# Product-key experts: both weight streams in 1 MB halves through six half places, where they were 2 MB pieces through three

## The chip, the cores and the metric

One Trainium2 chip, one of its cores. The program is written out instruction by instruction for five engines: TensorE (PE, matmul), VectorE (DVE), ScalarE (ACT), GpSimd (POOL) and SyncE (SP), which issues all loads. The metric is the device time of one launch in microseconds, lower is better.

## What is computed

The reference is two transformer blocks, one after another, in fp32 on 256 tokens of width 1024. The first has two layers, each a mixer (a gated linear recurrence beside sparse attention) and then product-key experts. The second has one layer with latent attention, a second recurrence and 32 gated experts. The change is about the product-key experts, which each of the first block's two layers computes so:

```
def _peer(x, wq, subkeys, u_tab, v_tab):
    ...
    q = (xf @ wq).reshape(T, PEER_HEADS, 2, PEER_KEY_DIM)
    s = jnp.einsum('thcd,ckd->thck', q, subkeys).astype(jnp.float32)
    sv, si = lax.top_k(s, PEER_TOPK)
    ...
    experts = (ea * PEER_KEYS + eb).reshape(T, PEER_HEADS * PEER_TOPK)
    gate = jax.nn.softmax(cv, axis=-1).reshape(T, PEER_HEADS * PEER_TOPK).astype(x.dtype)
    ...
    def one_chunk(args):
        xc, ec, gc = args
        act = jax.nn.gelu(jnp.einsum('cd,ced->ce', xc, u_tab[ec]))
        return jnp.einsum('ce,ced->cd', act * gc, v_tab[ec])
```

T is 256, there are 8 heads, 128 x 128 = 16384 experts and 16 chosen per head. u_tab and v_tab are 16384 x 1024 each, 64 MB a table and layer.

## The kernel before

The kernel does not gather. It reads both tables whole and computes all 16384 experts for all tokens, with a dense gate that is zero where an expert was not chosen. The experts go in 128 chunks of 128.

- The up product of a chunk (pe_stage1) is 8 fp32 matmuls of 256 columns, each of them two records in the trace: 16 records a chunk. ScalarE applies gelu and stores the 128 x 256 result in H, which holds 76 chunks (HELD).
- A build (pe_build) makes the gates of 32 chunks for 16 tokens from one-hot tables that VectorE writes (dve_keys_hot, dve_gates_hot): 48 small matmuls. VectorE then multiplies H by them (dve_gate). There are 64 builds a layer.
- The down product of a chunk (pe_stage2) is 12 matmuls of 512 columns. H and the v chunk are each split in a high part (ScalarE: act_split_p, act_split_v) and a low part (VectorE: dve_split_p, dve_split_v); v_hi has three buffers and v_lo two. So dve_split_v of chunk c waits for the down product of chunk c-2, and act_split_v for that of c-3.

The order of the work is written out by hand and is the same in all engines' programs. First come 50 up chunks (BEFORE), with the first 16 builds among the last 18 of them. Then there are 128 steps c = 0 to 127. Each does the builds due in it, the up chunks of first_at[c] and the down product of chunk c. first_at[c] is 50 + 2c and 51 + 2c as long as H has room (c up to 24), then one chunk a step, and none from c = 53 on. ScalarE and VectorE split chunk c + 2 in step c.

The weights pass through a ring in SBUF: NSLOT = 3 places of PIECE = 4096 columns, 2 MB each (class Slots, line 209). load() (line 300) takes the next place in turn, waits on SyncE until the load's predecessor in that place has been given back, and issues one DMA, which adds 16 to the place's own semaphore when it has landed. SyncE's program is in order: a load whose place is not free holds up every load behind it. All weights of the first block pass this ring, and in the mixed stretch of the steps both tables do. sp_u and sp_v (lines 957 and 961) load a piece of 4 chunks when their c is a multiple of 4; sp_peer has the order: in each step first the up pieces, then the down piece of chunk c + 2. An up piece is given back by TensorE after its fourth chunk (pe_stage1), a down piece by VectorE after the split of its fourth chunk (dve_split_v). A piece lies in memory as 128 rows of 16 KB.

In the second block's experts the ring gets more places in the arena (more_slots, line 2004).

Of the kernel before, what the change touches and what calls it, by code (L numbers as in the profile page):

```python
# [17 lines left out]
NSLOT = 3  # L18
PIECE = 4096
HELD = 76  # L20
# [211 lines left out]

def bc(ap, axis, n):
    ap = ap.unsqueeze(axis)
    shape = list(ap.shape)
    shape[axis] = n
    return ap.broadcast_to(shape)


def build(nc, d, out):  # L240
    with ExitStack() as ctx:
# [50 lines left out]

        ring = Slots([ring_t[:, i * PIECE:(i + 1) * PIECE] for i in range(NSLOT)], at)
        s_ring = [sem(f"ring{i}_landed") for i in range(NSLOT)]
        fills = [0] * NSLOT
# [4 lines left out]
        def load(src, cols, *key):  # L300
            buf, (s, n) = ring.take(*key)
            i = ring.place[key]
            fills[i] += 1
            S.wait_ge(s, n)
            S.dma(buf[:, 0:cols], src, s_ring[i])
            at.put(("landed", key), s_ring[i], 16 * fills[i])
# [136 lines left out]
        def pe_mod(j):  # L443
# [6 lines left out]
            w = ring.of("w_mod", j).rearrange("p (c n) -> p c n", c=8)  # L450
# [106 lines left out]
        def pe_project_out(l, k, yT, *made):  # L557
            P.wait_ge(*at[made])
            P.wait_ge(*at["landed", ("w_out", l, k)])
            w = ring.of("w_out", l, k).rearrange("p (c n) -> p c n", c=4)  # L560
# [8 lines left out]
        def pe_mixing(l):  # L569
# [5 lines left out]
            for j in range(4):  # L575
                P.wait_ge(*at["landed", ("w_inA", l, j)])
                w = ring.of("w_inA", l, j).rearrange("p (c n) -> p c n", c=8)
# [379 lines left out]
        def sp_u(l, c):  # L957
            if c % 4 == 0:
                load(d["peer_u"][l, c // 4], 4096, "u", l, c // 4)

        def sp_v(l, c):
            if c % 4 == 0 and c < 128:
                load(d["peer_v"][l, c // 4], 4096, "vt", l, c // 4)
# [15 lines left out]
        def pe_stage1(l, c):  # L979
            P.wait_ge(*at["landed", ("u", l, c // 4)])  # L980
            if c >= 2:
                P.wait_ge(*at["gelu", l, c - 2])
            w = ring.of("u", l, c // 4).rearrange("p (i c a) -> p i c a", i=4, c=8)
            P.mm(bU[c % 2][:, 0:256], [(w[:, c % 4, dc, :], xT[:, dc, :]) for dc in range(8)])
            P.mark("up", l, c)
            if c % 4 == 3:
                ring.back(P, "u", l, c // 4)
# [22 lines left out]
        def pe_peer(l):  # L1010
            after_stage(P, "mix", l)
            route_banks.restart()
            for j in range(4):
                P.wait_ge(*at["landed", ("wq", l, j)])
                w = ring.of("wq", l, j).rearrange("p (c n) -> p c n", c=8)
# [121 lines left out]
        def dve_split_v(l, c):  # L1137
            w = ring.of("vt", l, c // 4).rearrange("p (i n) -> p i n", i=4)[:, c % 4, :]
# [5 lines left out]
            if c % 4 == 3:  # L1144
                ring.back(V, "vt", l, c // 4)
# [74 lines left out]
        def act_split_v(l, c):  # L1220
            A.wait_ge(*at["landed", ("vt", l, c // 4)])
            if c >= 3:
                A.wait_ge(*at["down", l, c - 3])
            A.act(v_hi[c % 3], ring.of("vt", l, c // 4).rearrange("p (i n) -> p i n", i=4)[:, c % 4, :], ACT.Copy)
            A.mark("v high", l, c)
# [134 lines left out]
        def pe_task(kind, k, ct):  # L1360
            P.wait_ge(*at["landed", ("w_hg", kind, k)])
            w = ring.of("w_hg", kind, k).rearrange("p (c n) -> p c n", c=8)
# [115 lines left out]
        def pe_mixer():  # L1478
# [17 lines left out]
            w = ring.of("w_kvb").rearrange("p (v c n) -> p v c n", v=2, c=2)  # L1496
# [508 lines left out]
        s_ring += [sem(f"ring{NSLOT + i}_landed") for i in range(len(more_slots))]  # L2005
# [29 lines left out]
        def sp_moe():  # L2035
# [5 lines left out]
            for i in range(len(more_slots)):  # L2041
                ring.bufs.append(more_slots[i])
                ring.tenant.append(None)
                fills.append(0)
            ring.n = NSLOT
# [52 lines left out]
        def pe_up(j, i, k, *gathered):  # L2098
            x = xe[i]
            for v in range(2):  # L2100
# [7 lines left out]
                for h in range(2):  # L2108
                    P.wait_ge(*at["landed", ("w_gu", j, v, h)])
                    w = ring.of("w_gu", j, v, h).rearrange("p (c g n) -> p c g n", c=4, g=2)  # L2110
# [21 lines left out]
        def pe_down(j):  # L2132
# [3 lines left out]
            for hf in range(2):  # L2136
                P.wait_ge(*at["landed", ("w_dn", j, hf)])
                w = ring.of("w_dn", j, hf).rearrange("p (f n) -> p f n", f=4)
# [376 lines left out]
        def start_ring():  # L2515
            ring.bufs, fills[:] = ring.bufs[0:NSLOT], [0] * NSLOT
            ring.restart()
# [183 lines left out]
```

## Time and profile before

| | |
|---|---|
| median of 3 runs | 4375.6 us (4365.14 to 4375.74) |
| the profiled execution | 4377.6 us |
| its span | 4375.8 us |
| TensorE matmul busy | 3942.4 us (90%) |
| TensorE weight load busy | 2746.5 us (63%) |
| VectorE busy | 2018.1 us (46%) |
| ScalarE busy | 895.2 us (20%) |
| mean granted clock of TensorE | 0.944 |
| loads of each table | 64 of 2048 KB, 8.7 us (up) and 8.6 us (down) from issue to landing |

The mean over the span says little, since the stages have different limits. Times in the rows count from the span's start. Layer 0's experts run from about 240 to 1280 us, layer 1's from about 1490 to 2530 us, and the second block's experts from 3285 us to the end. Granted clock is the share of full speed (2.4 GHz) that TensorE was given. "Idle before" is the time in which an engine stood still before a row, with the one that released it.

### The profile page before, as it was taken

How to read it: one execution, taken by the hardware profiler on the slowest of the kernel's cores; microseconds unless marked ns; L12 is line 12 of the kernel's file. 1: busy time of each engine (PE TensorE's matmuls, PEld its weight loads, DVE VectorE, ACT ScalarE, POOL GpSimd, SP SyncE). 2: the span in 40 equal slices, each digit the busy share in tenths (PEclk: the TensorE clock that was granted, in tenths of full speed). 3: DMA queues.
4: the chain of work that ended last, by engine and by line, in shares of the span. 5: the costliest groups of instructions: out<-in, count | busy, mean ns of one | idle time of the engine just before them, and what ended most of it. 6: DMA issues, size and time to landing. Idle time of an engine off the chain costs nothing.

```text
span 4375.8 us, 54878 instructions
## 1 busy us (share of the span) xinstructions
PE 3942.4 (90%) x23468; PEld 2746.5 (63%) x23468; DVE 2018.1 (46%) x3441; ACT 895.2 (20%) x1502; POOL 154.4 (4%) x135
## 2 busy tenths in 40 slices
PE   6989999998988899999998979998869999999986
PEld 5778878886777688887876756565643333332333
DVE  4276645748754497255758533355532111111112
ACT  2311111223434111212233421223300000000000
POOL 0000000000000000000000000021200000000000
PEclk9799999999998899999999989999979999999998
DMA  4433323443344333333443331211129999999993
GB/s 182 155 135 138 132 116 131 159 155 135 135 165 155 134 137 125 124 136 135 154 154 123 137 127 49 106 58 58 58 81 413 427 428 427 428 427 428 425 398 145
DMA packets 62282, 846.18 MB, mean 193 GB/s; under 512 B 6800, under 2 KB 8976, under 8 KB 10160
## 3 DMA queue, kind: packets, MB, share of 16 engines
q1 hardware_dynamic: 62032, 842.60, 47.9%
q8 instruction: 187, 3.06, 0.3%
q14 instruction: 63, 0.52, 0.0%
HBM read 841.52 MB, written 1.05 MB: 193 GB/s over the span
## 4 chain that ended last, share of the span: by engine, by line
PE 67%; DVE 15%; DMA 13%; ACT 3%; issue 2%; SPq 0%; POOL 0%; DVEq 0%; ACTq 0%
PE bank L83 65%; DVE arena L119 6%; DMA ring<-in_w_gu_dram 6%; DMA ring<-in_peer_u_dram 3%; DMA arena<-in_w_gu_dram 3%; ACT arena L109 2%; DVE vlo L119 2%; PE bank L96 2%; DVE arena L187 1%; DVE arena L181 1%; DVE arena L193 1%; DVE arena L145 1%; DVE arena L133 1%; DVE arena L125 1%; DVE arena L127 1%
## 5 line engine op out<-in xcount | busy, mean ns | idle before, releaser
L83 PE MATMUL bank<-xT,ring 128*128 128x256 f32 x5120 | 1174.1, 389 | 55.7 <-DMA ring<-in_peer_u_dram 33.4
L83 PEld LDWEIGHTS bank<-xT,ring 128*128 128x128 f32 x5120 | 988.2, 195 | 197.8 <-DMA ring<-in_peer_u_dram 35.9
L83 PE MATMUL bank<-arena 128*128 128x32 bf16 (+7 forms) x9660 | 926.6, 291 | 145.7 <-DVE arena L119 108.5
L83 PEld LDWEIGHTS bank<-arena 128*128 128x128 bf16 (+4 forms) x9660 | 544.4, 126 | 522.9 <-issue 294.5
L83 PE MATMUL bank<-ring,arena 128*64 128x512 f32 (+1 forms) x2304 | 592.5, 606 | 39.5 <-DMA ring<-in_w_gu_dram 33.7
L109 ACT ACTIVATE arena<-bank 128x256 f32<-128x256 f32 (+2 forms) x484 | 223.8, 462 | 1975.2 <-PE bank L83 1484.6
L83 PEld LDWEIGHTS bank<-ring,arena 128*64 128x64 f32 (+1 forms) x2304 | 194.4, 146 | 427.3 <-issue 328.5
L119 DVE TENSOR_TENSOR arena<-arena 128x512 bf16<-128x512 bf16 (+6 forms) x636 | 424.4, 703 | 82.0 <-ACT arena L109 67.9
L119 DVE TENSOR_TENSOR vlo<-ring,vhi 128x1024 fp32r<-128x1024 f32 x256 | 313.2, 1224 | 267.2 <-PE bank L83 249.8
L83 PE MATMUL bank<-vhi,phi 128*128 128x512 f32 x1024 | 432.3, 422 | 0.0
L83 PE MATMUL bank<-vhi,plo 128*128 128x512 f32 x1024 | 406.7, 397 | 0.0
L83 PE MATMUL bank<-vlo,phi 128*128 128x512 f32 x1024 | 406.6, 397 | 0.0
L83 PE MATMUL bank<-arena,ring 128*128 128x256 f32 (+2 forms) x1472 | 363.3, 409 | 26.6 <-issue 14.2
L119 DVE TENSOR_TENSOR arena<-cst,arena 128x2048 bf16<-128x2048 f32 (+1 forms) x257 | 372.4, 1481 | 0.0
L83 PEld LDWEIGHTS bank<-arena,ring 128*128 128x128 f32 (+1 forms) x1472 | 253.1, 188 | 129.0 <-issue 91.4
L109 ACT ACTIVATE arena<-arena 128x512 f32<-128x512 f32 (+7 forms) x202 | 134.4, 666 | 797.8 <-DVE arena L125 619.0
L109 ACT ACTIVATE vhi<-ring 128x1024 fp32r<-128x1024 f32 x256 | 272.0, 1063 | 31.4 <-DMA ring<-in_peer_v_dram 20.3
L119 DVE TENSOR_TENSOR plo<-arena,phi 128x256 fp32r<-128x256 f32 x256 | 107.9, 421 | 318.2 <-ACT phi L109 318.2
L139 DVE COPY arena<-bank 128x256 f32<-128x256 f32 (+4 forms) x124 | 70.3, 567 | 387.9 <-PE bank L83 337.1
L83 PEld LDWEIGHTS bank<-vhi,plo 128*128 128x128 f32 x1024 | 197.1, 192 | 44.0
L83 PEld LDWEIGHTS bank<-vlo,phi 128*128 128x128 f32 x1024 | 198.0, 193 | 40.3
L83 PEld LDWEIGHTS bank<-vhi,phi 128*128 128x128 f32 x1024 | 197.5, 193 | 39.6
(105 smaller groups left out, 1665.9 us busy)
## 6 DMA issues: line engine op xcount, KB each, us to landing
ring<-in_w_gu_dram SPq DMA_DIRECT2D x85, 2048.0 KB, 19.3
ring<-in_peer_u_dram SPq DMA_DIRECT2D x64, 2048.0 KB, 8.7
ring<-in_peer_v_dram SPq DMA_DIRECT2D x64, 2048.0 KB, 8.6
arena<-in_w_gu_dram SPq DMA_DIRECT2D x55, 2048.0 KB, 19.4
ring<-in_w_dn_dram SPq DMA_DIRECT2D x41, 2048.0 KB, 17.9
arena<-in_w_dn_dram SPq DMA_DIRECT2D x29, 2048.0 KB, 20.6
ring<-in_w_hg_dram SPq DMA_DIRECT2D x14, 2048.0 KB, 8.6
ring<-in_w_mod_dram SPq DMA_DIRECT2D x12, 2048.0 KB, 7.8
```

The costliest lines, as they stand in the source:

```text
L83: i = self.e.matmul(o, l, r, start=start, stop=stop)
L96: self.e.transpose(o, src, ident[0:n, 0:n]).then_inc(self.sem, 1)
L109: self.e.activation(o, i, f, scale=scale, **kw).then_inc(self.sem, 1)
L119: self.e.tensor_tensor(o, a, b, op).then_inc(self.sem, 1)
L125: self.e.tensor_scalar(o, a, s1, None, o1).then_inc(self.sem, 1)
L127: self.e.tensor_scalar(o, a, s1, s2, o1, o2).then_inc(self.sem, 1)
L133: self.e.scalar_tensor_tensor(out=o, in0=a, scalar=s, in1=b, op0=o1, op1=o2).then_inc(self.sem, 1)
L139: self.e.tensor_copy(o, i).then_inc(self.sem, 1)
L145: self.e.tensor_reduce(o, i, AX.X, op, negate=neg).then_inc(self.sem, 1)
L181: self.e.max(o, i).then_inc(self.sem, 1)
L187: self.e.max_index(o, v, i).then_inc(self.sem, 1)
L193: self.e.match_replace(o, v, i, by).then_inc(self.sem, 1)
```

## The change

A new class Ring takes the place of Slots for the weight ring. It counts in half places. A load of up to 2048 columns takes one half, a wider one both halves of a place; where a wide load would start on a second half, that half is skipped. load() waits for all that the taken halves held before. Each half has its own landing semaphore (a wide load uses that of its first half). sp_u and sp_v load 2 chunks at a time, 1 MB as 128 rows of 8 KB, when their c is even; the halves are given back after every second chunk. All other loads of the ring keep their size and order. The readers of wide loads now slice the first 4096 columns, which is all that the parts left out here do beside the added places of the second block.

```
@@ -17,6 +17,7 @@
 ALPHA = 4.0 ** 0.25
 NSLOT = 3
 PIECE = 4096
+HALF = PIECE // 2
 HELD = 76
 TURNED = 19
 BEFORE = 50
...
@@ -225,6 +226,37 @@
 
     def of(self, *key):
         return self.bufs[self.place[key]] if key in self.place else self.bufs[0]
+
+    def back(self, q, *key):
+        self.at.put(("back", key), q.sem, q.n)
+
+
+class Ring:
+
+
+    def __init__(self, places, at):
+        self.places, self.at, self.place = list(places), at, {}
+        self.restart()
+
+    def restart(self):
+        self.n, self.tenant = 0, [None] * (2 * len(self.places))
+
+    def take(self, cols, *key):
+        wide = cols > HALF
+        if wide and self.n % 2:
+            self.n += 1
+        i = self.n % len(self.tenant)
+        self.n += 1 + wide
+        before = [k for k in self.tenant[i:i + 1 + wide] if k]
+        self.tenant[i:i + 1 + wide] = [key] * (1 + wide)
+        self.place[key] = i
+        return i, [self.at["back", k] for k in before]
+
+    def half(self, i):
+        return self.places[i // 2][:, i % 2 * HALF:]
+
+    def of(self, *key):
+        return self.half(self.place.get(key, 0))
 
     def back(self, q, *key):
         self.at.put(("back", key), q.sem, q.n)
...
@@ -290,19 +322,19 @@
         def par(c, n=1):
             return pp[:, c:c + n]
 
-        ring = Slots([ring_t[:, i * PIECE:(i + 1) * PIECE] for i in range(NSLOT)], at)
-        s_ring = [sem(f"ring{i}_landed") for i in range(NSLOT)]
-        fills = [0] * NSLOT
+        ring = Ring([ring_t[:, i * PIECE:(i + 1) * PIECE] for i in range(NSLOT)], at)
+        s_ring = [sem(f"ring{i}_landed") for i in range(2 * NSLOT)]
+        fills = [0] * (2 * NSLOT)
         banks = Slots(bank, at)
         s_landed = {}
         s_out = sem("out_stored")
 
         def load(src, cols, *key):
-            buf, (s, n) = ring.take(*key)
-            i = ring.place[key]
+            i, before = ring.take(cols, *key)
             fills[i] += 1
-            S.wait_ge(s, n)
-            S.dma(buf[:, 0:cols], src, s_ring[i])
+            for s, n in before:
+                S.wait_ge(s, n)
+            S.dma(ring.half(i)[:, 0:cols], src, s_ring[i])
             at.put(("landed", key), s_ring[i], 16 * fills[i])
 
         def once(dst, src, *key):
...
@@ -447,7 +479,7 @@
             P.wait_ge(s, n)
             P.wait_ge(*at["landed", ("w_mod", j)])
             P.wait_ge(*at["silu c"])
-            w = ring.of("w_mod", j).rearrange("p (c n) -> p c n", c=8)
+            w = ring.of("w_mod", j)[:, 0:PIECE].rearrange("p (c n) -> p c n", c=8)
             for dc in range(8):
                 for g in range(4):
                     P.one(b[32 * g:32 * g + 32, 0:128], sc[:, dc, :], w[:, dc, g * 128:g * 128 + 128],
...
@@ -955,12 +987,12 @@
                 build_at.setdefault(b + 1, []).append(n)
 
         def sp_u(l, c):
-            if c % 4 == 0:
-                load(d["peer_u"][l, c // 4], 4096, "u", l, c // 4)
+            if c % 2 == 0:
+                load(d["peer_u"][l, c // 4][:, c % 4 * 1024:c % 4 * 1024 + 2048], 2048, "u", l, c // 2)
 
         def sp_v(l, c):
-            if c % 4 == 0 and c < 128:
-                load(d["peer_v"][l, c // 4], 4096, "vt", l, c // 4)
+            if c % 2 == 0 and c < 128:
+                load(d["peer_v"][l, c // 4][:, c % 4 * 1024:c % 4 * 1024 + 2048], 2048, "vt", l, c // 2)
 
         def sp_peer(l):
             for j in range(4):
...
@@ -977,14 +1009,14 @@
 
 
         def pe_stage1(l, c):
-            P.wait_ge(*at["landed", ("u", l, c // 4)])
+            P.wait_ge(*at["landed", ("u", l, c // 2)])
             if c >= 2:
                 P.wait_ge(*at["gelu", l, c - 2])
-            w = ring.of("u", l, c // 4).rearrange("p (i c a) -> p i c a", i=4, c=8)
-            P.mm(bU[c % 2][:, 0:256], [(w[:, c % 4, dc, :], xT[:, dc, :]) for dc in range(8)])
+            w = ring.of("u", l, c // 2)[:, 0:HALF].rearrange("p (i c a) -> p i c a", i=2, c=8)
+            P.mm(bU[c % 2][:, 0:256], [(w[:, c % 2, dc, :], xT[:, dc, :]) for dc in range(8)])
             P.mark("up", l, c)
-            if c % 4 == 3:
-                ring.back(P, "u", l, c // 4)
+            if c % 2:
+                ring.back(P, "u", l, c // 2)
 
         def pe_build(l, n):
             ah, bh = Aoh[n % 2], Boh[n % 2]
...
@@ -1135,14 +1167,14 @@
             V.mark("p split", l, c)
 
         def dve_split_v(l, c):
-            w = ring.of("vt", l, c // 4).rearrange("p (i n) -> p i n", i=4)[:, c % 4, :]
+            w = ring.of("vt", l, c // 2)[:, c % 2 * 1024:c % 2 * 1024 + 1024]
             V.wait_ge(*at["v high", l, c])
             if c >= 2:
                 V.wait_ge(*at["down", l, c - 2])
             V.tt(v_lo[c % 2], w, v_hi[c % 3].bitcast(F32), SUB, lag=FREE)
             V.mark("v split", l, c)
-            if c % 4 == 3:
-                ring.back(V, "vt", l, c // 4)
+            if c % 2:
+                ring.back(V, "vt", l, c // 2)
 
         def dve_peer(l):
             after_stage(V, "mix", l)
...
@@ -1218,10 +1250,10 @@
             A.mark("p high", l, c)
 
         def act_split_v(l, c):
-            A.wait_ge(*at["landed", ("vt", l, c // 4)])
+            A.wait_ge(*at["landed", ("vt", l, c // 2)])
             if c >= 3:
                 A.wait_ge(*at["down", l, c - 3])
-            A.act(v_hi[c % 3], ring.of("vt", l, c // 4).rearrange("p (i n) -> p i n", i=4)[:, c % 4, :], ACT.Copy)
+            A.act(v_hi[c % 3], ring.of("vt", l, c // 2)[:, c % 2 * 1024:c % 2 * 1024 + 1024], ACT.Copy)
             A.mark("v high", l, c)
 
         def act_peer(l):
...
@@ -2038,11 +2070,11 @@
             S.wait_ge(*at["bd cleared"])
             once(bd[0:32, :], d["b_dn"], "b_dn")
             once(bgu[0:32, :], d["b_gu"], "b_gu")
-            for i in range(len(more_slots)):
-                ring.bufs.append(more_slots[i])
-                ring.tenant.append(None)
-                fills.append(0)
-            ring.n = NSLOT
+            for place in more_slots:
+                ring.places.append(place)
+                ring.tenant += [None, None]
+                fills.extend([0, 0])
+            ring.n = 2 * NSLOT
             load(d["w_gu"][0, 3], 4096, "w_gu", 0, 1, 1)
             for j in range(1, 33):
                 if j < 32:
...
@@ -2513,7 +2545,7 @@
             pool_moe()
 
         def start_ring():
-            ring.bufs, fills[:] = ring.bufs[0:NSLOT], [0] * NSLOT
+            ring.places, fills[:] = ring.places[0:NSLOT], [0] * (2 * NSLOT)
             ring.restart()
 
 
```

## Rows read from the trace of the kernel before

**Rows 1.** The page: the chain's shares by line; GB/s in 40 slices.
```profile
PE bank L83 65%; DVE arena L119 6%; DMA ring<-in_w_gu_dram 6%; DMA ring<-in_peer_u_dram 3%; DMA arena<-in_w_gu_dram 3%; ACT arena L109 2%; DVE vlo L119 2%; PE bank L96 2%; DVE arena L187 1%; DVE arena L181 1%; DVE arena L193 1%; DVE arena L145 1%; DVE arena L133 1%; DVE arena L125 1%; DVE arena L127 1%
...
GB/s 182 155 135 138 132 116 131 159 155 135 135 165 155 134 137 125 124 136 135 154 154 123 137 127 49 106 58 58 58 81 413 427 428 427 428 427 428 425 398 145
```

**Rows 2.** Waits of PE at 526-822, 1776-2074, 995-1160: us in total, times, longest.
```profile
PE bank L83 <- DMA ring<-in_peer_u_dram: 16.0, 6, 5.1
PE bank L83 <- DVE arena L119: 2.8, 1, 2.8
...
PE bank L83 <- DMA ring<-in_peer_u_dram: 17.4, 6, 5.1
PE bank L83 <- DVE arena L119: 2.7, 1, 2.7
...
PE bank L83 <- DVE arena L119: 28.0, 16, 2.2
```

**Rows 3.** Timeline of PE, layer 0: start us, us, instructions xcount [idle before <-releaser].
```profile
490.25 1.40 PE L83 MATMUL bank<-arena 128*128 128x32 bf16 x48 [4.07 <-DVE arena L119]
...
525.31 7.07 PE L83 MATMUL bank<-xT,ring 128*128 128x256 f32 x32
...
535.64 7.17 PE L83 MATMUL bank<-xT,ring 128*128 128x256 f32 x32 [0.50 <-DMA ring<-in_peer_u_dram]
...
628.06 8.60 PE L83 MATMUL bank<-xT,ring 128*128 128x256 f32 x32 [2.62 <-DMA ring<-in_peer_u_dram]
...
676.00 10.21 PE L83 MATMUL bank<-xT,ring 128*128 128x256 f32 x32 [2.51 <-DMA ring<-in_peer_u_dram]
...
820.48 1.35 PE L83 MATMUL bank<-arena 128*128 128x32 bf16 x48 [2.80 <-DVE arena L119]
821.68 5.39 PE L83 MATMUL bank<-xT,ring 128*128 128x256 f32 x16
```

**Rows 4.** Timeline of all engines ahead of the wait at 820.48.
```profile
796.24 3.70 PE L83 MATMUL bank<-xT,ring 128*128 128x256 f32 x16
...
804.05 0.33 SPq L206 DMA_DIRECT2D ring<-in_peer_v_dram  x1
...
812.62 1.06 ACT L109 ACTIVATE vhi<-ring 128x1024 fp32r<-128x1024 f32 x1 [4.30 <-DMA ring<-in_peer_v_dram]
813.71 1.23 DVE L119 TENSOR_TENSOR vlo<-ring,vhi 128x1024 fp32r<-128x1024 f32 x1 [3.94 <-ACT vhi L109]
```

**Rows 5.** Timeline of all engines, 565 to 582 us: one stall for an up piece.
```profile
565.05 1.23 DVE L119 TENSOR_TENSOR vlo<-ring,vhi 128x1024 fp32r<-128x1024 f32 x1 [1.55 <-PE bank L83]
566.30 0.33 SPq L206 DMA_DIRECT2D ring<-in_peer_v_dram  x1
566.68 5.53 SPq L206 DMA_DIRECT2D ring<-in_peer_u_dram  x2
...
574.87 1.06 ACT L109 ACTIVATE vhi<-ring 128x1024 fp32r<-128x1024 f32 x1 [2.14 <-DMA ring<-in_peer_v_dram]
...
579.76 2.50 PE L83 MATMUL bank<-xT,ring 128*128 128x256 f32 x5 [5.15 <-DMA ring<-in_peer_u_dram]
```

**Rows 6.** Loads by source and size, KB each, median us from issue to landing.
```profile
ring<-in_cmp_w_dram SPq DMA_DIRECT2D x4, 1024.0 KB, 4.8
ring<-in_ln_dram SPq DMA_DIRECT2D x4, 1024.0 KB, 6.1
...
arena<-in_alibi_dram SPq DMA_DIRECT2D x2, 1024.0 KB, 7.1
```

**Rows 7.** Windows: us, then busy of PE, PEld, DVE, ACT, POOL; granted clock; DMA share; GB/s.
```profile
386.00:400.00 14.00, 14.00 (x67) 12.32 (x66) 0.00 (x0) 1.54 (x4) 0.00 (x0) 1.00 0.39 150
623.00:671.00 48.00, 45.38 (x370) 38.87 (x369) 27.80 (x32) 9.01 (x16) 0.00 (x0) 0.96 0.33 133
820.00:995.00 175.00, 174.52 (x1328) 148.81 (x1329) 106.46 (x139) 47.17 (x77) 0.00 (x0) 0.99 0.40 149
1158.00:1262.00 104.00, 103.72 (x492) 85.60 (x492) 56.91 (x74) 51.79 (x69) 0.00 (x0) 0.98 0.50 188
```

More of the change, by code:

```diff
@@ L559, in pe_project_out @@
             P.wait_ge(*at["landed", ("w_out", l, k)])
-            w = ring.of("w_out", l, k).rearrange("p (c n) -> p c n", c=4)
+            w = ring.of("w_out", l, k)[:, 0:PIECE].rearrange("p (c n) -> p c n", c=4)
             for tk in range(2):
@@ L576, in pe_mixing @@
                 P.wait_ge(*at["landed", ("w_inA", l, j)])
-                w = ring.of("w_inA", l, j).rearrange("p (c n) -> p c n", c=8)
+                w = ring.of("w_inA", l, j)[:, 0:PIECE].rearrange("p (c n) -> p c n", c=8)
                 for half in range(2):
@@ L1014, in pe_peer @@
                 P.wait_ge(*at["landed", ("wq", l, j)])
-                w = ring.of("wq", l, j).rearrange("p (c n) -> p c n", c=8)
+                w = ring.of("wq", l, j)[:, 0:PIECE].rearrange("p (c n) -> p c n", c=8)
                 for hf in range(2):
@@ L1361, in pe_task @@
             P.wait_ge(*at["landed", ("w_hg", kind, k)])
-            w = ring.of("w_hg", kind, k).rearrange("p (c n) -> p c n", c=8)
+            w = ring.of("w_hg", kind, k)[:, 0:PIECE].rearrange("p (c n) -> p c n", c=8)
             cs = slice(ct * 128, ct * 128 + 128)
@@ L1495, in pe_mixer @@
             P.wait_ge(*at["ckv"])
-            w = ring.of("w_kvb").rearrange("p (v c n) -> p v c n", v=2, c=2)
+            w = ring.of("w_kvb")[:, 0:PIECE].rearrange("p (v c n) -> p v c n", v=2, c=2)
             for h in range(8):
@@ L2004, in build @@
         more_slots = [ar(PIECE) for _ in range((ARENA - top[0]) // PIECE)]
-        s_ring += [sem(f"ring{NSLOT + i}_landed") for i in range(len(more_slots))]
+        s_ring += [sem(f"ring{2 * NSLOT + i}_landed") for i in range(2 * len(more_slots))]
         top[0] = e_mark
@@ L2109, in pe_up @@
                     P.wait_ge(*at["landed", ("w_gu", j, v, h)])
-                    w = ring.of("w_gu", j, v, h).rearrange("p (c g n) -> p c g n", c=4, g=2)
+                    w = ring.of("w_gu", j, v, h)[:, 0:PIECE].rearrange("p (c g n) -> p c g n", c=4, g=2)
                     for c in range(4):
@@ L2137, in pe_down @@
                 P.wait_ge(*at["landed", ("w_dn", j, hf)])
-                w = ring.of("w_dn", j, hf).rearrange("p (f n) -> p f n", f=4)
+                w = ring.of("w_dn", j, hf)[:, 0:PIECE].rearrange("p (f n) -> p f n", f=4)
                 for f in range(4):
```

## The prediction

> **What bounds the kernel now.** I read the views in this order: the page's chain, the chain in order of time, the waits of the matmul queue by stretch, then timelines of single stalls. The chain's shares by line say that matmuls (line 83) are 65% of the span and the up table's transfers (ring<-in_peer_u_dram) 3% [rows 1]. The reader should not take 3% for the gain: a transfer stands on the chain with its whole length, though TensorE works through most of it. The loss is TensorE's idle time. In the mixed stretch (steps c = 0 to 24, each with two chunks of the up product and one of the down product, and the few steps behind them that one late piece still reaches: 526 to 822 us in layer 0 and 1776 to 2074 us in layer 1), the matmul queue sat idle for up-table transfers 6 times each, 16.0 and 17.4 us, and once each for VectorE at the end, 2.8 and 2.7 us [rows 2]. Together 38.9 us.
>
> The two single waits look like a VectorE matter. The rows around the first, at 820.48 [rows 3], say otherwise: the down piece was issued at 804.05, ScalarE waited 4.30 us for it and began its split at 812.62, VectorE waited 3.94 us for ScalarE's half of the split, and so made the one-hot tables of the next build late [rows 4]. It is the same ring, one wait further on.
>
> The stalls have a second cost. The 32 matmul records of a step's up product take 7.17 us at 535.64, where the engine had hardly stopped. After the ten longer stalls they take 8.60 to 8.86 us (seven of them, as at 628.06) or 9.93 to 10.21 us (three, as at 676.00); after the stall at 820.48 the 16 records of one chunk take 5.39 us [rows 3] where at 796.24 they take 3.70 [rows 4], and after its like in layer 1 nothing is added. The granted clock says why: 0.96 over 623 to 671 us against 0.99 over 820 to 995 us and 1.00 over 386 to 400 us, where it does not stop [rows 7], so for a few us the engine ran at 1.2 in place of 2.4 GHz. Extra time: 7 x 1.65 + 3 x 2.95 + 1.69 = 22.1 us.
>
> **Why these stalls come.** Each load goes into the next place of the ring, and the transfer queue of SyncE issues in program order: a load whose place is not free holds all behind it. In the mixed stretch the order is two up pieces, one down piece; with three places each down piece therefore takes the place of the down piece before it. That is free only when VectorE has split its last chunk, 4k-1, and this split waits for the down product of chunk 4k-3 (two v_lo buffers). The rows show it: v_lo of that chunk at 565.05 to 566.28, the down load at 566.30, the up load behind it at 566.68 [rows 5]. The down piece lands 8.57 us after issue (ScalarE starts on it at 574.87 after waiting 2.14 us), the up piece 13.1 us (TensorE goes on at 579.76). TensorE wanted the up piece at the next step's start, 0.85 of a step after 566.30. A step lasts 9.8 us (525.31 to 535.64, less 0.50 of idle time), and a build adds 1.2 us (820.48 to 821.68) [rows 3]. So the lead is 8 to 9 us and the need 13.
>
> **The change, part by part.**
>
> *Places.* With halves the order in the mixed stretch is up, up, down over two steps, and with six half places a load takes the place of the load six before it, which is the down half two earlier, or the up half four earlier. Down half m (chunks 2m, 2m+1) can be issued once chunk 2m-3 is split, that is 0.15 of a step into step 2m-4. ScalarE wants it in step 2m-2 at about 0.75: a lead of 2.6 steps in place of 0.6. The up half behind it is wanted at the start of step 2m-1: 2.85 steps in place of 0.85. At 9.8 us a step or more that is 25 to 28 us. Landing: the 1 MB loads of the trace took 4.8, 6.1 and 7.1 us [rows 6]; with another before it in the queue I add 2.4 us, half of the 4.8 us that the second 2 MB piece added (579.7 less 566.68 is 13.0, less 8.57, plus the 0.38 us between issues). Even 9.5 us is under 25. So all twelve up waits and both late down pieces go: minus 38.9 us.
>
> *Clock.* With the stalls go the slowed matmuls behind them: minus 22.1 us. I take the whole, since 175 us of unbroken matmuls (820 to 995 us) ran at 0.99 [rows 7]; the other end is 0, if something else lowers the clock as often.
>
> *Entering and leaving the mixed stretch.* The first down half may be issued two halves of the up stream earlier, but the 4.07 us that TensorE waits at 490.25 [rows 3] come from VectorE's own order (it splits two chunks ahead of a build's tables), not from the load; nothing is counted. Where one up chunk and one down chunk make a step (820 to 995 us), there were no transfer waits and the six half places hold the same bytes: nothing.
>
> *More instructions.* Per layer 64 more loads on SyncE, 0.33 us each on a queue whose gaps are tens of us: hidden by its waits for places. TensorE waits for 32 more landings per layer and ScalarE for 32. Of the landing wait the trace has a direct sign: in the stretch with up chunks alone, one each 3.45 us, every fourth has such a wait, and over 386 to 400 us TensorE is busy 14.00 of 14.00 us [rows 7]. So a wait for data that is there costs under 0.01 us; 128 of them at most 1.3 us, and 0 is taken. Behind a landing wait on TensorE stands the whole step, which would matter only if the half were late.
>
> *Smaller transfers.* Rows become 8 KB in place of 16 KB. What has to be served fastest is the last stretch, with down chunks alone: 41 chunks (492 records of 12) in about 104 us [rows 7], one half per 5.06 us. If loads overlap in flight as the 2 MB ones do, a half adds 2.4 us and nothing shows. If halves came strictly one after another at the 6.1 us of the 1 MB row for ln, 1.04 us x 20.5 halves x 2 layers = 43 us would be given back; at 4.8 us none; at 7.1 us 84 us. I take 0, since the two 2 MB loads of [rows 5] overlap, and in the expert phase 2 MB loads arrive at 428 GB/s [rows 1].
>
> The Trainium skill has a rule against this part ("DMA: Bandwidth & Descriptors", Measured): batch transfers to at least 1 MiB for 75% of peak, with 6.15 us and 341 GB/s for 1 MB from GpSimd's queue. The halves sit at that knee. As an estimate by its 6.15 us, taken serially, 45 us would be given back and the sum would be 16 us. No row here shows several 1 MB loads in flight; the rival below prices it by rows.
>
> *Everything else.* Loads over 2048 columns take both halves of a place and skip a left-over half, so the mixers, the second block and its experts use the same places in the same order. Their times stay.
>
> **Sum.** 38.9 + 22.1 = 61.0 us. The profiled execution took 4377.6 us with a span of 4375.8; the median of the runs is 4375.6, so I take 61.0 from the median as it is: 4314.6 us. The likeliest case has its own range, 4308 to 4325, for the waits' cost, a dip or two of the clock that stays, and a stall of a few us that remains.
>
> **Rivals.**
>
> *The clock does not come back (4337 us).* The idle time goes, but dips stay: 38.9 alone. For it: TensorE also stops for VectorE, once for 4.07 us just before the mixed stretch, and any such stop can lower the clock. Against: none in the 175 us without stalls.
>
> *VectorE's chain takes the stalls' place (4376 us, no change).* TensorE waits for VectorE 28.0 us in all in 995 to 1160 us [rows 2], so near the mixed stretch this chain is a bound already: v split of chunk c+2 waits for down product c. If it needed more than a step, each freed us would turn into a VectorE wait. Against: VectorE is busy 27.8 of 48 us [rows 7], and between the stalls steps follow without idle time: 7 waits are all there are in 296 us [rows 2].
>
> *Halves served one after another, mildly (4358 us).* 43 us given back as above, at 6.1 us a half.
>
> *The same, worse: slower than before (4399 us).* One mechanism: the 1 MB loads do not overlap and need 7.1 us each, as the alibi row has it, so that the last stretch, which needs a half per 5.06 us, becomes bound by transfers: 84 us given back against 61 won. It decides from (61.0 / 41) + 5.06 = 6.55 us a half on. For it: two of the three 1 MB rows are over 5.06 us. Against: these are times to landing, not spacings, and 2 MB pieces overlap.
>
> **How the numbers follow.** The forecast 0.80, clock 0.07, VectorE 0.06, mild serial 0.04, slower 0.03. What is under 0.3% (13 us) can't be told from no change here. Faster by more: 0.80 + 0.07 + 0.04 = 0.91; same 0.06; slower 0.03. Range 4303 to 4342: the forecast's own, widened below for dips counted too small and above to take in the clock case.
>
> **What would show it.** Right: no wait of TensorE for ring<-in_peer_u_dram in either mixed stretch, none of ScalarE for in_peer_v_dram there, all steps' 32 records at about 7.15 us, granted clock 0.99 or more between 530 and the end of the single-chunk stretch, up and down halves issued some 25 us before use, the last stretch still about 104 us for 492 records. Wrong: waits that stay with a new name (VectorE, ScalarE's v_hi), halves landing at more than 6.55 us spacing, gaps or a lower clock in the last stretch, or an expert phase (from 3285 us) that is longer than its 1091 us.

## The result

The changed kernel takes 4300.2 us (median of 4 runs, 4291.4 to 4306.8) against 4374.7 us of the kernel before: ratio 0.9833, 95% interval 0.981 to 0.9856. Repeated twice beside other kernels it gave 4297.1 against 4369.0 us (0.9837, 0.9824 to 0.985) and 4294.1 against 4367.2 us (0.9836, 0.9822 to 0.9849). It is faster by 72 to 75 us. The forecast was 61.0 us and 4314.6 us with a range down to 4303; the time lies 2.8 us below that range. The direction and the place were right, and 11 to 14 us came from places that I had called unchanged.

### The profile page after: what moved, and what is told of

It is laid out like the page before. It is cut to its first block, busy times and chain, and to the rows that moved or that the text cites. A ratio compares the mean times of both kernels' runs of the same rounds, so it can differ in the third digit from the quotient of the medians.

```text
span 4296.2 us, 55136 instructions
## 1 busy us (share of the span) xinstructions
PE 3901.6 (91%) x23468; PEld 2716.2 (63%) x23468; DVE 2017.5 (47%) x3441; ACT 893.2 (21%) x1502; POOL 154.0 (4%) x135
## 4 chain that ended last, share of the span: by engine, by line
PE 71%; DVE 15%; DMA 9%; ACT 3%; issue 2%; POOL 0%; SPq 0%; DVEq 0%; ACTq 0%
PE bank L84 70%; DVE arena L120 6%; DMA ring<-in_w_gu_dram 6%; DMA arena<-in_w_gu_dram 2%; ACT arena L110 2%; PE bank L97 2%; DVE arena L188 1%; DVE vlo L120 1%; DVE arena L182 1%; DVE arena L194 1%; DVE arena L146 1%; DVE arena L134 1%; DVE arena L126 1%; DVE arena L128 1%; DVE arena L152 0%
## 5 line engine op out<-in xcount | busy, mean ns | idle before, releaser
L84 PE MATMUL bank<-xT,ring 128*128 128x256 f32 x5120 | 1150.4, 383 | 22.4 <-DMA mq<-in_mq_dram 18.8
L84 PEld LDWEIGHTS bank<-xT,ring 128*128 128x128 f32 x5120 | 972.3, 192 | 155.4 <-issue 20.9
L84 PEld LDWEIGHTS bank<-vhi,phi 128*128 128x128 f32 x1024 | 197.2, 193 | 39.8
```

The costliest lines, as they stand in the source:

```text
L84: i = self.e.matmul(o, l, r, start=start, stop=stop)
```

## The profile after

The page: busy times, the chain's shares by line, and the loads of the two tables (KB each, median us to landing). Line numbers are one higher than before.

```profile
PE 3901.6 (91%) x23468; PEld 2716.2 (63%) x23468; DVE 2017.5 (47%) x3441; ACT 893.2 (21%) x1502; POOL 154.0 (4%) x135
...
PE bank L84 70%; DVE arena L120 6%; DMA ring<-in_w_gu_dram 6%; DMA arena<-in_w_gu_dram 2%; ACT arena L110 2%; PE bank L97 2%; DVE arena L188 1%; DVE vlo L120 1%; DVE arena L182 1%; DVE arena L194 1%; DVE arena L146 1%; DVE arena L134 1%; DVE arena L126 1%; DVE arena L128 1%; DVE arena L152 0%
...
ring<-in_peer_u_dram SPq DMA_DIRECT2D x128, 1024.0 KB, 5.2
ring<-in_peer_v_dram SPq DMA_DIRECT2D x128, 1024.0 KB, 5.2
```

The up table has left the chain, where it had 3% [rows 1]. A half lands after 5.2 us, between the rows of [rows 6]. The chain in order of time (start us, us, what) shows the whole of what [rows 2] counted as 38.9 us of waits:

```profile
365.03 108.70 PE bank L84 x1008
475.31 2.36 DVE vlo L120 x2
477.67 2.81 DVE arena L120 x2
482.55 472.64 PE bank L84 x3612
...
1119.74 103.76 PE bank L84 x492
...
1700.88 472.72 PE bank L84 x3612
...
2334.01 102.13 PE bank L84 x492
```

From 482.55 to 955 us, and again in layer 1, 3612 records follow each other as one piece of the chain, in which TensorE waits for nothing. Before, six transfers of the up table and one of the down table cut each such stretch. The last piece of a layer, 492 records (the 48 of one build and 444 of 37 down chunks), is as long as it was [rows 7]: the smaller loads cost nothing there. Seven of its loads on SyncE, in the timeline over 1119 to 1160 us, are issued 5.44 us apart (32.67 us over six), more than a half's 5.2 us to landing:

```profile
1126.90 33.00 SPq L207 DMA_DIRECT2D ring<-in_peer_v_dram  x7
```

The wait of 4.07 us at 490.25 [rows 3] is still there, ahead of 482.55.

The windows (us, then busy of PE, PEld, DVE, ACT, POOL, granted clock, DMA share, GB/s) say the same of the clock:

```profile
483.00:743.00 260.00, 260.00 (x1970) 224.59 (x1966) 134.88 (x158) 53.62 (x97) 0.00 (x0) 0.99 0.42 150
743.00:933.00 190.00, 190.00 (x1534) 162.42 (x1534) 127.40 (x164) 49.21 (x80) 0.00 (x0) 1.00 0.43 150
1120.00:1224.00 104.00, 103.49 (x488) 85.32 (x484) 56.87 (x73) 51.62 (x69) 0.00 (x0) 0.98 0.51 178
```

TensorE is busy in every us of the first two. Its timeline, to be read against [rows 3], has 7.07 us for each step's 32 records, with no idle time ahead, and the issue queue is far ahead:

```profile
536.86 7.07 PE L84 MATMUL bank<-xT,ring 128*128 128x256 f32 x32
546.54 7.07 PE L84 MATMUL bank<-xT,ring 128*128 128x256 f32 x32
...
563.32 0.33 SPq L207 DMA_DIRECT2D ring<-in_peer_u_dram  x1
577.10 0.33 SPq L207 DMA_DIRECT2D ring<-in_peer_v_dram  x1
577.47 6.83 SPq L207 DMA_DIRECT2D ring<-in_peer_u_dram  x2
598.99 0.33 SPq L207 DMA_DIRECT2D ring<-in_peer_v_dram  x1
...
609.65 7.15 PE L84 MATMUL bank<-xT,ring 128*128 128x256 f32 x32
```

The down half issued at 577.10, in step 8, is for chunks 12 and 13, which ScalarE wants in step 10. The up half right behind it is for step 11, whose up records start at 609.65, 32 us later. Before, the up piece was issued 8 us ahead of its use and landed 13 us after issue, 5 too late [rows 5]. Loads overlap: of two halves issued 0.37 us apart the second lands 2.5 us behind the first (median of 31 pairs, from the trace's landing times).

**Where the time went, by stretch.** Taken from the start times of the matmul records that bound each stretch, in us; steps 0 to 52 count from the first down product. Behind the slash stands the time lost to slow clock: half of the length of the clock's records at half speed. It counts time in which TensorE stood idle too, so it is the most that can have been lost. Two profiles of the kernel before (the second is r_before, below) and three of the changed one:

| stretch | before, two profiles | changed, three profiles |
|---|---|---|
| first mixer and routing, layer 0 | 286.6 / 42.7, 281.4 / 37.5 | 278.8 / 34.1, 284.7 / 39.3, 278.9 / 34.1 |
| first 50 up chunks, layer 0 | 199.1 / 1.7, 199.1 / 1.7 | 199.0 / 1.7, 199.1 / 1.7, 199.0 / 1.7 |
| steps 0 to 52, layer 0 | 481.6 / 11.9, 479.2 / 11.9 | 450.1 / 0, 450.1 / 0, 450.1 / 0 |
| steps 53 to 91, layer 0 | 169.5 / 13.7, 166.2 / 10.2 | 170.4 / 13.7, 166.9 / 10.2, 164.5 / 6.8 |
| steps 0 to 52, layer 1 | 482.6 / 11.9, 479.5 / 10.2 | 450.1 / 0, 450.1 / 0, 450.1 / 0 |
| steps 53 to 91, layer 1 | 166.5 / 11.9, 172.5 / 17.1 | 164.6 / 6.8, 164.6 / 6.8, 168.2 / 11.9 |
| mixer and routing, layer 1 | 283.0 / 39.8, 285.3 / 42.7 | 282.7 / 39.6, 282.8 / 39.7, 278.5 / 35.8 |
| second block | 1856.9 / 104.1, 1850.7 / 97.6 | 1850.3 / 99.1, 1846.8 / 92.3, 1846.5 / 93.8 |

Steps 0 to 52 gained 31.5 + 32.5 = 64.0 us against the first profile and 29.1 + 29.4 = 58.5 against the second: 61.3 on average. What is beyond that, 16 us between the mean spans, is in the other rows: 4 us in steps 53 to 91, 6 in the two mixers, 6 in the second block. These rows also differ from profile to profile of one and the same kernel, together with their slow-clock time.

Five profiles are few, but the span and the granted clock of every run are on record, and span x (1 - clock) is the lost time of the table for the whole run. It is 238 us on average over 47 runs of the kernel before and 201 us over 14 of the changed one. Of these 37 us about 23 are in steps 0 to 52; so 14 us of slow clock went elsewhere, about as much as the time beyond the forecast.

## The experiments

### The two kernels again: r_before and r_after

No edit.

> The kernel before once more, unchanged, to see how much of it moves by itself. Of the 79.6 us between the two profiled spans, 64.0 lie between the 490.25 us mark of layer 0 and the end of the down products of both layers; 7.7 lie ahead of layer 0's up products and 6.6 in the second block, in stretches that the change does not touch. Theory A (the slow-clock stretches of the mixers fall as they happen to fall): this second profile of the same kernel differs from the first in those stretches by several us either way, while the mixed stretches again show 16 and 17 us of waits. Theory B (the change makes the mixers faster too): the mixers here take what they took in the first profile, within 1 us. Both expect 4374 us in the median.

Measured: 4367.2 us (12 runs) against 4369.0 us of before (17 runs) measured beside it, ratio 1.0002 (0.9993 to 1.0012); single runs from 4358.6 to 4374.6. The profile has 281.4 us in the first mixer where the first had 286.6, and 15.7 + 15.7 us of waits in the two stretches of two-chunk steps.

> The changed kernel once more, unchanged. Theory A: the mixers differ from the first profile of it by several us, the product-key stretches are the same within 1 us; the median against before comes out between 60 and 80 us, 64 if the luck is even. Theory B: the mixers are again 8 and 7 us faster than those of the kernel before, and the median difference is 75 to 80 us.

Measured: 4297.1 us, 71.9 us faster. Steps 0 to 52 are 450.1 us in both layers again, to the tenth, and the first mixer took 284.7 us, 5.9 more than in the first profile. Theory A holds for the mixers: they move by themselves with their slow-clock time. But the medians are not 64 us apart. Two things follow. My base, 4375.6 us from three runs, was high by 7 us for this kernel; and about 10 us of the difference are not in the mixed stretches and not mere scatter of single runs.

### The order alone: e_order

```diff
             sp_v(l, 0)
+            for i in first_at[0]:
+                sp_u(l, i)
             for c in range(128):
-                for i in first_at[c]:
+                for i in first_at.get(c + 1, ()):
                     sp_u(l, i)
                 sp_v(l, c + 2)
```

> The kernel before with 2 MB pieces and three places; only the order of issue changes, each step's up piece is issued ahead of the down piece of the step before. Theory 1 (the up piece was late because it stood in the queue behind a down piece that waited for its place): its lead grows from 0.85 to 2.3 steps, all twelve up waits go (33.4 us and 20.4 us of slow matmuls), the two late down pieces stay (5.5 us, 1.7 us): 4374 - 54 = 4320 us. Theory 2 (what counts is that a smaller load lands sooner): nothing lands sooner here, 4374 us.

Measured: 4302.5 us, ratio 0.9847 (0.9833 to 0.986), 66.5 us faster. Steps 0 to 52 take 450.1 us in both layers, exactly as with halves. The timeline of the issue queue:

```profile
606.89 0.33 SPq L206 DMA_DIRECT2D ring<-in_peer_v_dram  x1
613.77 22.22 SPq L206 DMA_DIRECT2D ring<-in_peer_u_dram  x2
650.68 0.33 SPq L206 DMA_DIRECT2D ring<-in_peer_v_dram  x1
657.56 22.22 SPq L206 DMA_DIRECT2D ring<-in_peer_u_dram  x2
...
765.73 0.33 SPq L206 DMA_DIRECT2D ring<-in_peer_v_dram  x1
```

No up piece stands within 0.4 us behind a down piece, as at 566.68 in [rows 5]; the down piece is alone, ScalarE waits for it (7.6 us in six waits in layer 0), and TensorE does not. Theory 2 is out: no load got smaller. I had left the late down piece of 804.05 [rows 4] in the sum; it went too. Its counterpart is at 765.73, and since the step products begin at 512.7 us in both profiles and 26.8 us of stalls are gone, it is issued 12 us earlier. Counted through the new order of takes, it gets the place of an up piece, which TensorE gives back in step 24, and not that of the down piece before it. The kernel is 17 us faster than theory 1 said: 7 us are these down pieces, 5 my base, and 5 lie outside steps 0 to 52. So the whole gain in these stretches was to be had without smaller loads, by the order of issue alone.

### Landing alone: e_landing

```diff
+        def load2(src, *key):
+            buf, (s, n) = ring.take(*key)
...
+            S.dma(buf[:, 0:2048], src[:, 0:2048], s_ring[i])
...
+            S.dma(buf[:, 2048:4096], src[:, 2048:4096], s_second[i])
```

> The kernel before with three places of 2 MB, given back whole as before, but each filled by two 1 MB loads with a landing semaphore each, so that a piece's first half can be used while its second is in flight. Theory 1 (places and queue set the issue time, which stays): the first half lands about 2.4 us sooner than the piece did, so the up waits of 5.1 us shrink to 2.7 and those of 2.4 to 3.3 us to 0 to 0.9, in sum 8 of 33.4 us, the waits of 2.8 us for the down piece to 0.4; minus 30 us for the idle time, and up to 22 more for the clock: 4322 to 4344 us. Theory 2 (sooner landing alone is the whole effect): no waits left, 4310 us as the changed kernel has by its product-key stretches.

Measured: 4311.9 us, ratio 0.9868 (0.9853 to 0.9883), 57.1 us faster, above the 52 us that theory 1 allowed and 2 us off theory 2's time, though not all waits went. The waits of PE (us in total, times, longest), 483 to 940 us:

```profile
PE bank L83 <- DVE arena L119: 4.1, 1, 4.1
PE bank L83 <- DMA ring<-in_peer_u_dram: 1.8, 1, 1.8
```

One up wait a layer is left, 1.8 and 1.6 us, where I had worked out 2.7, and the others are gone; behind it no matmul is slow. So the two-chunk steps take 262.1 and 261.9 us, against 260.1 in the changed kernel. The waits shrank more than forecast, since the first half of an up piece behind a down piece lands 9.2 us after issue (the load of 567.35 us in this trace), where the whole piece took 13.0. A sooner first half and an earlier issue are each enough almost by themselves, since the stalls were short against what either gives: 3.3 us or less but for one a layer. The effects of the two do not add.

### Half the ring: e_near3

```diff
+        if key[0] in ("u", "vt"):
+            before += self.late[-3:-3 + 1 or None][:1] if len(self.late) >= 3 else []
+            self.late.append(key)
+        else:
+            self.late = []
```

> The changed kernel, in which an up or down half also waits until the third load before it in the stream is given back, so that it works as with three half places (3 MB) in place of six (6 MB). Theory 1 (what counts is lead against landing, not how many bytes the ring holds): the up half that stands behind a down half has again a lead of 0.85 steps, 8.2 us, or 9.3 with a build, but both are 1 MB and land after about 5.2 + 2.4 = 7.6 us, so it just fits: no up waits or some tenths of a us, within 5 us of the changed kernel, 70 us faster than before. Theory 2 (the six places themselves are the gain): half the ring brings back waits as large as before or larger: 4369 us or more.

Measured: 4316.3 us, ratio 0.9882 (0.9865 to 0.9899), 54 us faster than before and about 20 slower than the changed kernel. In the two-chunk steps theory 1 is right: 260.1 us in both layers, no wait. Its total (within 5 us of the changed kernel) is not. The loss is where I had not looked, at the entry. Waits of PE over 440 to 940 us, then the timeline:

```profile
PE bank L84 <- DVE arena L120: 9.0, 1, 9.0
PE bank L84 <- DMA ring<-in_peer_u_dram: 0.5, 2, 0.3
```

```profile
481.16 0.33 SPq L207 DMA_DIRECT2D ring<-in_peer_v_dram  x1
486.51 2.14 ACT L110 ACTIVATE vhi<-ring 128x1024 fp32r<-128x1024 f32 x2 [4.96 <-DMA ring<-in_peer_v_dram]
487.59 2.36 DVE L120 TENSOR_TENSOR vlo<-ring,vhi 128x1024 fp32r<-128x1024 f32 x2 [6.16 <-ACT vhi L110]
...
494.83 1.44 PE L84 MATMUL bank<-arena 128*128 128x32 bf16 x48 [8.95 <-DVE arena L120]
```

VectorE wants the first down half in the middle of the first sixteen builds, long before the first down product. With three half places it is issued only then, and its tables for the next build are late: 5.8 and 4.1 us more in this stretch, 2.3 and 2.6 more behind step 24, where up waits of up to 0.5 us come back. That is 15 of the 20 us; where the rest is was not found. The lead has to be counted where the order asks for the data first.

### The wait at the thirteenth build: v_split

```diff
-                if n == 12:
-                    dve_split_v(l, 0)
-                    dve_split_v(l, 1)
             dve_gate(l, 15)
             dve_split_p(l, 0)
+            dve_split_v(l, 0)
             dve_split_p(l, 1)
+            dve_split_v(l, 1)
```

> The changed kernel with VectorE's first two splits of the down table moved from the 13th of the first sixteen builds to behind the 16th. The 4.07 us wait of TensorE at the 13th build goes in both layers, with 1.5 us of slow clock behind each: 11 us faster than the changed kernel (81 us faster than before). Rival: VectorE needs 5.3 us a build there and TensorE 4.7, so the wait only comes a build or two later and smaller: 3 to 6 us faster.

Measured: 4291.3 us, ratio 0.9826 (0.9811 to 0.9841), 79 us faster than before. The first 50 up chunks take 194.5 us in place of 199.1, in both layers: 0.9 us of waits in place of 4.1 and no slow clock. That is 9.2 us. But the steps 53 to 91 took 171.6 and 171.4 us with 15.4 us of slow clock in each, more than in any profile of the changed kernel, and the profiled span is 4298.0 us, the longest of its five runs. Over the five runs the lost time is 207 us on average, where the changed kernel has 201, though 3 us of it are gone from the up stretch. So an edit 470 us earlier seems to have moved slow clock in stretches whose instructions are the same; one profile does not prove it for this one.

### Filling the stops: e_fill

```diff
                 for n in build_at.get(c, ()):
+                    if n >= 48:
+                        P.wait_ge(*at["gelu", l, 127])
+                        for k in range(FILLED):
+                            P.one(bU[0][:, 0:256], ident, xT[:, k, :], True, True, False)
                     pe_build(l, n)
```

> The changed kernel with three matmuls whose result is not used (1.3 us at full clock) ahead of each of the last sixteen builds of a layer, where TensorE waits about 1.8 us for VectorE. They take place in time that is idle already. Theory A (what the change gave beyond the mixed stretches is clock in other stretches, which falls after TensorE's stops): the slow-clock time of this tail, 10.2 and 6.8 us in the last profile of the changed kernel, goes to 0 to 3 us a layer, and the kernel is 8 to 15 us faster than the changed one. Theory B (the tail's length is VectorE's alone and a lower clock of TensorE there costs nothing): the clock record rises, the time stays within 3 us.

Measured: 4284.0 us, ratio 0.9809 (0.9794 to 0.9823), 86 us faster than before, and 10 to 16 us faster than the three medians of the changed kernel. The steps 53 to 91 take 159.0 and 158.9 us, with no slow clock in either layer. The same two stops of TensorE, first in r_after, then here with the added matmuls (they read xT and cst):

```profile
1019.18 1.35 PE L84 MATMUL bank<-arena 128*128 128x32 bf16 x48 [2.24 <-DVE arena L120]
...
1027.61 1.35 PE L84 MATMUL bank<-arena 128*128 128x32 bf16 x48 [1.49 <-DVE arena L120]
```

```profile
1017.16 1.46 PE L85 MATMUL bank<-xT,cst 128*128 128x256 f32 x6
1019.56 1.35 PE L85 MATMUL bank<-arena 128*128 128x32 bf16 x48 [0.94 <-DVE arena L121]
1026.34 1.46 PE L85 MATMUL bank<-xT,cst 128*128 128x256 f32 x6
1027.99 1.35 PE L85 MATMUL bank<-arena 128*128 128x32 bf16 x48 [0.19 <-DVE arena L121]
```

And this stretch in windows of v_split, r_after and e_fill, in this order; the clock is the third number from the end:

```profile
965.00:1130.00 165.00, 139.08 (x1176) 112.36 (x1175) 137.24 (x166) 54.69 (x74) 0.00 (x0) 0.91 0.34 116
```

```profile
966.00:1122.00 156.00, 127.86 (x1155) 103.53 (x1153) 137.14 (x167) 54.69 (x74) 0.00 (x0) 0.95 0.37 124
```

```profile
968.00:1117.00 149.00, 141.17 (x1250) 116.17 (x1248) 136.17 (x166) 54.70 (x74) 0.00 (x0) 1.00 0.38 129
```

VectorE's busy time is the same 136 to 137 us in all three; the clock goes from 0.91 over 0.95 to 1.00 and the stretch gets shorter. Theory B is out: slow matmuls of TensorE lengthen a stretch that looks like VectorE's, since VectorE's splits wait for down products (17.2 us in ten waits in the window of r_after, 11.3 us in six in that of e_fill). In 18 such stretches without filling (nine profiles) the time runs from 164.5 us with 6.8 lost to 172.5 us with 17.1 lost, 0.8 us for each us lost. The straight line through them reaches 158.6 us where nothing is lost, and the filled stretches take 159.0.

### VectorE's work to GpSimd: v_pool

```diff
-                    dve_split_p(l, c + 2)
+                    if c + 2 < POOLED:
+                        dve_split_p(l, c + 2)
...
+            for c in range(POOLED, 128):
+                pool_split_p(l, c)
```

> The kernel of v_split in which GpSimd, idle in this stage, makes the low part of the gated chunk (plo, 0.42 us each on VectorE) from chunk 55 on. VectorE loses 1.0 of its 9.5 us per build in the tail, where TensorE needs 7.8: if VectorE's busy time sets the pace, 16 x 1.0 us a layer and some clock, 25 to 40 us faster than v_split. Rival: GpSimd takes over 2.7 us a chunk (TensorE's time for one), or slows VectorE beside it, and the tail becomes longer by 0.5 to 1 us a chunk, 40 to 70 us slower.

Measured: 4340.2 us, ratio 0.9937 (0.9922 to 0.9952): 49 us slower than v_split. The steps 53 to 91 take 190.2 and 193.1 us. The split's rows by tile (ns min/median/max, first and last start), and one stretch of the timeline:

```profile
L121 POOL TENSOR_TENSOR plo<-arena,phi x146: 959/1401/1751, 961.7 to 2476.7; 128x256 fp32r<-128x256 f32 x146
L121 DVE TENSOR_TENSOR plo<-arena,phi x110: 414/425/427, 505.3 to 2191.4; 128x256 fp32r<-128x256 f32 x110
```

```profile
1011.63 1.40 POOL L121 TENSOR_TENSOR plo<-arena,phi 128x256 fp32r<-128x256 f32 x1 [7.62 <-ACT phi L111]
...
1012.35 1.23 DVE L121 TENSOR_TENSOR arena<-cst,arena 128x512 bf16<-128x512 f32 x1
```

GpSimd takes 1.40 us where VectorE took 0.42, and VectorE's own comparison beside it takes 1.23 us, where alone it takes 0.68. The rival's price was right. Of its two reasons the rows show the second, that VectorE gets slower beside GpSimd; GpSimd itself stays under the 2.7 us a chunk. Its durations in a profile are rough, and no run has it without VectorE beside it, so how much of the 1.40 us is its own is not shown.

### The filled pair: e_fillb, e_fill2 and r_after2

e_fillb is the kernel before with the three matmuls of e_fill; e_fill2 and r_after2 have no further edit.

> The kernel before (2 MB pieces, three places) with the three unused matmuls ahead of each of the last sixteen builds of a layer. In e_fill they took the slow clock out of this tail: 158.9 us in both layers. Theory A (of the 9 us by which the change beat its 61 us in the mixed stretches, the tail gave a part, by where its slow-clock stretches fell): the tail is 159 us here too, this kernel is 18 to 20 us faster than before (mean tail 168.7), and e_fill beats it by 61 to 66 us. Theory B (the 9 us come from elsewhere): e_fill beats it by 70 us or more.

> The kernel of e_fill again, as partner of e_fillb on the same chip. Tails of 159 us in both layers, about 84 us faster than before, 61 to 66 us faster than e_fillb by theory A, 70 or more by theory B.

> The changed kernel unchanged, on the same chip as the three others: 70 us faster than before, with the tails between 164 and 172 us and the mixed stretches at 450.1 us in both layers.

Measured (all of this group beside each other): e_fillb 4344.2 us, ratio 0.9947 (0.9933 to 0.9961); e_fill2 4285.3 us, ratio 0.9807 (0.9793 to 0.982); r_after2 4294.1 us. The steps 53 to 91 take 159.0 us in both layers of both filled kernels. With them filled, the change is worth 58.9 us by the medians (61.3 by the means of five runs each); without, 73.1 us (74.2 by the means). By the scatter of the runs each of these is uncertain by about 5 us. Filling gives the kernel before 23 us, where 18 to 20 were forecast, and the changed one 9 us. Theory B (70 us or more) is out, and the excess over 61 us goes away when this clock is filled, as theory A has it. Where it sat is less clear. The profiles have 2 us a layer of it in the stretch that is filled, and the lost time over all runs differs by 31 us in the filled pair (213 and 182 us), 24 of them in steps 0 to 52. So of the 14 us of slow clock that differed elsewhere, filling took away about half.

### The two edits together: v_best

The diffs of v_split and e_fill together.

> The changed kernel with the two edits that helped: VectorE's first two splits of the down table behind the sixteenth build (4.6 us a layer in the profile of v_split) and the three unused matmuls ahead of each of the last sixteen builds. If both act alone: e_fill less 9 us, about 93 us faster than before, 4276 us. Rival: the shift of time brings slow clock elsewhere, as v_split's tails of 171.5 us did, and the gain is 84 us as in e_fill.

Measured: 4270.2 us (4268.8 to 4282.2), ratio 0.9788 (0.9771 to 0.9804): 97 us faster than before and 24 faster than the changed kernel beside it. It beats e_fill and v_split, and the forecast for two edits that act alone was 93 us. First 50 up chunks 194.5 us, steps 0 to 52 450.1 us, steps 53 to 91 158.9 us, in both layers. Two pieces of its chain in layer 0, the steps up to the first stop and the last down products:

```profile
486.82 466.49 PE bank L85 x3548
1108.04 102.13 PE bank L85 x492
```

The edits add up. In steps 53 to 91 the stops left are of at most 0.9 us, and no slow clock follows them, so the shift of time found nothing there to move.

## Why the prediction was wrong, step by step

- **What bounds it, and why the stalls come: right.** e_order takes nothing away but the place of the up piece behind the down piece, and all twelve waits go.
- **Places: right, and one cause more than needed.** Leads came out as forecast (25 to 28 us worked out, 32 us at 577.47, where builds lengthen the steps), and no wait is left. But the smaller landing (e_landing), the order (e_order) and half the places with small loads (e_near3) each do nearly all of it in the two-chunk steps. That six places were the cause can't be said; any one of three does.
- **Idle 38.9 and clock 22.1 us in the mixed stretches: right.** 61.0 forecast, 64.0 and 58.5 by the two profiles of before, 61.3 on average; the slow-clock part measured 23.8 and 22.1 us.
- **More instructions, smaller transfers: right.** 450.1 us without a gap, and the last 492 records in 102 to 104 us as before. A half landed 5.2 us after issue, the second of a pair 2.5 us behind the first (2.4 worked out), and the last stretch was served at 178 GB/s. The rule of the Trainium skill to batch transfers to at least 1 MiB ("DMA: Bandwidth & Descriptors", Measured) is just met by halves of 1 MB, so no run here tests what is below it; the 45 us estimated from its 6.15 us did not come, with 97.7 us for the last 36 down products in every profile, of the kernel before and of the changed one.
- **The need of the last stretch: misread, without effect on the sum.** The 492 records are the 48 of a build and 444 of 37 down products, not 41 of them. A half is needed every 5.4 us, as the issues 5.44 us apart show, not every 5.06. At the prediction's own landing times the two serial rivals would have given back 25 and 62 us in place of 43 and 84, so that the worse one would have meant no change, not a slower kernel.
- **"Everything else. Their times stay.": this step failed.** I took the steps 53 to 91, the mixers and the second block as fixed and put their change at nothing, though the trace of before has a granted clock of 0.94 over 995 to 1055 us and 0.92 over 1055 to 1160, where TensorE stops for VectorE at each build. Outside steps 0 to 52 the five profiles have 193 to 222 us of slow-clock time, about half of it in the second block. Over all runs this time fell by 14 us with the change, and the kernel gained 11 to 14 us more than the 61. With the slow clock taken out of steps 53 to 91 the change is worth 59 to 61 us, without 73.
- **The range: too narrow on the low side.** It gave 12 us below the forecast, worked out from the mixed stretches alone. Single runs of the kernel before already span 17 us, and the median of three runs that I subtracted from stood 7 us above that of 17. With the base of 17 runs the same sum would have said 4308 us, still 8 to 14 us above the measured medians.
- **The rivals.** None came: VectorE did not take the stalls' place in the mixed stretches, halves do overlap, and the clock did come back, even beyond what I counted.

What stays open: why the stretches outside steps 0 to 52 have less slow clock in the changed kernel, whose instructions there are the same but for the size of the loads, and how the 14 us divide between them. That steps 53 to 91 hold a part follows from the filled pair; the first mixer and the second block, where profiles of one kernel differ by up to 6 us, were not filled.

## What to carry to other kernels

In an in-order issue queue, a load inherits the wait of the load in front of it: compare for each stream the lead (from the event that frees its place to its first use, anywhere in the order) with issue to landing plus what stands ahead, and first try the order, which costs nothing. When a stop of TensorE goes, count the slow matmuls behind it as well; and for stretches that keep their stops, give the forecast a range for their slow clock, since it differed here between runs of one kernel and between kernels with the same instructions in them. Matmuls without a use, in time that is idle anyway, are a cheap way to find out what the clock costs there, and here to win it.

## What the runs showed of the hardware

- Slow clock costs time also where VectorE seems to set the pace: 0.8 us for each us lost, and 159.0 us without slow clock against 164.5 to 172.5 with 6.8 to 17.1 us lost.
- A stretch of 450 us in which TensorE never stops keeps its time to 0.1 us over nine profiles and both layers (the changed kernel three times, e_order, v_split, v_pool, e_fill, e_fill2, v_best), while steps 53 to 91, with a stop of 1.3 to 2.2 us at each build, differ by 6 us between profiles of the same kernel (166.2 to 172.5 before, 164.5 to 170.4 changed).
- VectorE is slower beside GpSimd: its 128x512 bf16 comparison took 1.23 us in place of 0.68. A 128x256 subtraction took 0.96 to 1.75 us on GpSimd, by the profile, against 0.42 on VectorE.
- Two 1 MB loads issued 0.37 us apart landed 2.5 us apart, each alone about 5.1 us after issue.
